# The square sums of the RMS norms and layer norms, taken with tokens on partitions and spread back to rows

## The reference, cut to what matters

```
def _rmsnorm(x, g):
    xf = x.astype(jnp.float32)
    xf = xf * lax.rsqrt(jnp.mean(xf * xf, axis=-1, keepdims=True) + EPS)
    return xf.astype(x.dtype) * g

def _layernorm(x, g, b):
    xf = x.astype(jnp.float32)
    mu = jnp.mean(xf, axis=-1, keepdims=True)
    xc = xf - mu
    var = jnp.mean(xc * xc, axis=-1, keepdims=True)
    return (xc * lax.rsqrt(var + EPS)).astype(x.dtype) * g + b
...
    for l in range(DEPTH):
        h = _rmsnorm(x, p["g_norm_mix"][l]) * (1 + scale_m) + shift_m
        m, st = _token_mixer(h, ...)          # its layer norm: conf = silu(_layernorm(conv, ...))
        x = x + gate_m * m
        h = _rmsnorm(x, p["g_norm_ffn"][l]) * (1 + scale_f) + shift_f
        f = _swiglu(h, ...) if l % 2 == 0 else _moe_swiglu(h, ...)
        x = x + gate_f * f
    y = _rmsnorm(x, p["g_final"])
```

## Time and profile before

| | |
|---|---|
| median of 3 runs | 1502.15 us (1499.78 to 1505.53) |
| the profiled execution: its own time, its span | 1501.98 us, 1500.2 us |
| PE busy | 1403.1 us, 94% of the span, 9312 products |
| PE weight loads busy | 1234.5 us, 82% |
| DVE busy | 1022.5 us, 68% |
| ACT busy | 785.6 us, 52% |
| DMA | 327.33 MB, mean 218 GB/s |
| granted clock of TensorE, mean | 0.968 of full speed |

### The profile page before, as it was taken

One profiled execution on the slowest core, in us unless ns is written; L12 is line 12 of the kernel. 1 busy time (PEld: TensorE's weight loads), 2 busy tenths in 40 slices (PEclk: granted clock), 3 DMA queues, 4 the chain that ended last, 5 costly groups with the idle time before them and its releaser, 6 DMA issues.

```text
span 1500.2 us, 24401 instructions
## 1 busy us (share of the span) xinstructions
PE 1403.1 (94%) x9312; PEld 1234.5 (82%) x9312; DVE 1022.5 (68%) x1417; ACT 785.6 (52%) x1062; POOL 38.2 (3%) x66
## 2 busy tenths in 40 slices
PE   5899999998889999998999999988899999999984
PEld 4788999875889999996989988767588888888863
DVE  2376999874554444334769987744788898889855
ACT  2534448634433333225443586243778788778852
POOL 0000100000000000000001000000200000000100
PEclk8999999999989999999999999999899999999996
DMA  9856743124446867434858661245689999999951
GB/s 310 228 169 197 235 141 125 59 85 154 135 140 201 255 217 237 177 100 121 246 159 290 198 186 57 85 140 188 223 320 386 383 387 388 378 386 385 384 203 68
DMA packets 280099, 327.33 MB, mean 218 GB/s; under 512 B 32319, under 2 KB 190471, under 8 KB 280007
## 3 DMA queue, kind: packets, MB, share of 16 engines
q1 hardware_dynamic: 273042, 314.29, 63.0%
q10 hardware_dynamic: 5492, 6.53, 1.3%
q0 software_dynamic: 1472, 5.24, 1.0%
HBM read 310.84 MB, written 15.17 MB: 217 GB/s over the span
## 4 chain that ended last, share of the span: by engine, by line
PE 88%; DVE 5%; ACT 2%; DMA 2%; SPq 1%; issue 1%; ACTq 0%; POOLq 0%; POOL 0%; DVEq 0%
PE mmp L819 14%; PE mmp L821 14%; PE mmp L820 13%; PE mmp L1221 8%; PE mmp L1223 8%; PE mmp L1222 8%; PE mmp L813 7%; PE py L789 2%; PE px L869 2%; PE py L885 1%; PE lg L985 1%; PE lg L869 1%; PE px L1027 1%; DVE hT L1796 1%; DMA ring<-in_w_ada_dram 1%
## 5 line engine op out<-in xcount | busy, mean ns | idle before, releaser
L819 PE MATMUL mmp<-hT_hi,wm_hi 128*128 128x320 f32 (+1 forms) x976 | 308.3, 316 | 13.1 <-DVE merged_lo L2023 5.1
L821 PE MATMUL mmp<-hT_hi,ring_lo 128*128 128x320 f32 (+1 forms) x976 | 306.2, 314 | 0.0
L820 PE MATMUL mmp<-hT_lo,wm_hi 128*128 128x320 f32 (+1 forms) x848 | 263.3, 310 | 0.0
L1827 DVE TENSOR_TENSOR ring_lo<-ring,wm_hi 128x1024 fp32r<-128x1024 f32 (+1 forms) x124 | 148.1, 1201 | 86.5 <-ACT wm_hi L1423 84.3
L819 PEld LDWEIGHTS mmp<-hT_hi,wm_hi 128*128 128x128 f32 (+1 forms) x976 | 184.7, 189 | 18.6 <-issue 8.4
L821 PEld LDWEIGHTS mmp<-hT_hi,ring_lo 128*128 128x128 f32 (+1 forms) x976 | 184.3, 189 | 0.2
L1423 ACT CAST wm_hi<-ring 128x1024 fp32r<-128x1024 f32 (+1 forms) x124 | 126.7, 1029 | 101.5 <-PE mmp L821 80.7
L820 PEld LDWEIGHTS mmp<-hT_lo,wm_hi 128*128 128x128 f32 (+1 forms) x848 | 159.3, 188 | 0.2
L1380 ACT ACTIVATE tmp<-mmp 128x320 f32<-128x320 f32 x70 | 30.7, 438 | 231.5 <-PE mmp L821 163.1
L1915 DVE SCALAR_TENSOR_TENSOR conv<-u_conf,dwc,conv 128x350 f32<-128x350 f32 x240 | 132.2, 581 | 3.1
L2048 DVE TENSOR_TENSOR wd_lo<-ring,wd_hi 128x2048 fp32r<-128x2048 f32 (+1 forms) x34 | 75.7, 2229 | 64.6 <-ACT wd_hi L1587 64.5
(11 more groups left out here) (371 smaller groups left out, 2866.2 us busy)
## 6 DMA issues: line engine op xcount, KB each, us to landing
ring<-in_w_in_dram SPq DMA_DIRECT2D x104, 512.0 KB, 4.6
ring<-in_w_exp_in_dram SPq DMA_DIRECT2D x64, 512.0 KB, 8.2
more<-in_w_exp_in_dram SPq DMA_DIRECT2D x64, 512.0 KB, 11.2
ring<-in_w_ada_dram SPq DMA_DIRECT2D x56, 512.0 KB, 7.2
more<-in_w_exp_out_dram SPq DMA_DIRECT2D x48, 512.0 KB, 6.9
ring<-in_w_ffn_in_dram SPq DMA_DIRECT2D x44, 512.0 KB, 5.9
wide<-in_w_ada_dram SPq DMA_DIRECT2D x40, 512.0 KB, 7.6
ring<-in_w_branch_dram SPq DMA_DIRECT2D x48, 256.0 KB, 2.8
```

Source lines behind the costliest of these rows:

```text
L819: nc.tensor.matmul(out, w_hi, x_hi, start=is_first, stop=False)
L820: nc.tensor.matmul(out, w_hi, x_lo, start=False, stop=False)
L821: return nc.tensor.matmul(out, w_lo, x_hi, start=False, stop=is_last)
L1827: V.tensor_tensor(mix_rows(ring_lo, l, s, r), mix_rows(ring, l, s, r), mix_hi(l, s, r).bitcast(F32), ALU.subtract).then_inc(mix_lo_ready, 1)
```

## The change

The sums are taken with tokens on partitions. For each squared block TensorE loads the squares as weights, for 64, 128 and 128 tokens in that order, and multiplies by one column of ones; the sums of 320 tokens stand in three columns of `py`. A product of zeros clears the columns first. ACT takes the root of these columns in two instructions (128x2 and 64x1), DVE the reciprocal of 128x3. Then TensorE spreads: for each column, it is repeated along the row as weights and multiplied by the identity, which gives `rstd` for each token on every partition, in PSUM (`rstd_rows`). DVE's multiplies read it there.

The spread of norm 0 stands behind the first transpose of the adaLN part; those of the others directly behind the sums. In the layer norm the spread stands ahead of chunk 2, and the multiply is moved behind the second merge. One memset on POOL is added at the start; `rstd` (1280 bytes on each partition) goes, and two tiles of 12 bytes come. `std` stays, as the router uses it.

```
+        sum_col = py[:, 0:3]
+        rstd_rows = py[:, P:P + T]
+        blocks_of = ((0, P), (P, P), (2 * P, TS))
...
+            nc.gpsimd.memset(std_col[:], 1.0)
...
+            def column_sums(squares, is_first, is_last):
+
+                if is_first:
+                    nc.tensor.matmul(sum_col, zeros[:, 0:P], zeros[:, 0:3], start=True, stop=False)
+                for t in (2, 0, 1):
+                    t0, m = blocks_of[t]
+                    ins = nc.tensor.matmul(py[0:m, t:t + 1], squares[:, t0:t0 + m], ones[:, 0:1],
+                                           start=False, stop=(is_last and t == 1))
+                return ins
+
+            def spread():
+
+                for t, (t0, m) in enumerate(blocks_of):
+                    ins = nc.tensor.matmul(rstd_rows[:, t0:t0 + m], rstd_col[0:m, t:t + 1].broadcast_to([m, P]),
+                                           ident[0:m, 0:m], start=True, stop=True)
+                return ins
...
-                    ins = nc.tensor.matmul(py[:, 0:T], ones[:], sq(k)[:, c, :], start=(c == 0), stop=(c == DC - 1))
+                    ins = column_sums(sq(k)[:, c, :], c == 0, c == DC - 1)
...
+            def norm_spread(k):
+                pe.wait_ge(rstd_ready, k + 1)
+                spread().then_inc(rstd_spread, 1)
...
             for m in range(ADA_FIRST):
                 ada_turn(0, m)
+                if m == 0:
+                    norm_spread(0)
...
                     norm_sums(2 * l)
+                    norm_spread(2 * l)
...
                     if j == 1:
                         pe.wait_ge(ln_sq, l + 1)
-                        group(py[:, 0:T], [(ones[:], hT[:, BC + c, :]) for c in range(BC)]).then_inc(ln_ss, 1)
+                        for c in range(BC):
+                            ins = column_sums(hT[:, BC + c, :], c == 0, c == BC - 1)
+                        ins.then_inc(ln_ss, 1)
+                    if j == 2:
+                        pe.wait_ge(ln_rstd, l + 1)
+                        spread().then_inc(ln_spread, 1)
...
+            def root_columns(n):
+                for m, c in ((P, slice(0, 2)), (TS, slice(2, 3))):
+                    ins = nc.scalar.activation(std_col[0:m, c], sum_col[0:m, c], ACT.Sqrt, scale=1.0 / n,
+                                               bias=eps[0:m, 0:1])
+                return ins
...
-                link(V.reciprocal(rstd[:], std[:]))
+                V.reciprocal(rstd_col[:], std_col[:]).then_inc(rstd_ready, 1)
...
             def norm_apply(k):
+                dve.wait_ge(rstd_spread, k + 1)
...
-                        V.tensor_tensor(hT[:, c, :], xT[:, c, :], rstd[:], ALU.mult).then_inc(xn_step, 1)
+                        V.tensor_tensor(hT[:, c, :], xT[:, c, :], rstd_rows, ALU.mult).then_inc(xn_step, 1)
...
-                        link(V.reciprocal(rstd[:], std[:]))
-                        V.tensor_tensor(hT[:, 0:BC, :], hT[:, 0:BC, :], bcast(rstd[:], BC, T),
+                        V.reciprocal(rstd_col[:], std_col[:]).then_inc(ln_rstd, 1)
+                    if j == 1:
+                        dve.wait_ge(ln_spread, l + 1)
+                        V.tensor_tensor(hT[:, 0:BC, :], hT[:, 0:BC, :], bcast(rstd_rows, BC, T),
                                         ALU.mult).then_inc(ln_n, 1)
```

More of the change, by code:

```diff
@@ L199, in build @@
         std = sb("std", [P, T])
-        rstd = sb("rstd", [P, T])
+        std_col = sb("std_col", [P, 3])
+        rstd_col = sb("rstd_col", [P, 3])
         vec = sb("vec", [P, DEPTH, NROWS])
@@ L408, in build @@
         std_ready = sem("std_ready")
+        rstd_ready = sem("rstd_ready")
+        rstd_spread = sem("rstd_spread")
         xn_step = sem("xn_step")
@@ L436, in build @@
         ln_std = sem("ln_std")
+        ln_rstd = sem("ln_rstd")
+        ln_spread = sem("ln_spread")
         ln_n = sem("ln_n")
@@ L1116, in _ @@
                 norm_sums(2 * l + 1, (DC - 2, DC - 1))
+                norm_spread(2 * l + 1)
                 if l % 2 == 0:
@@ L1278, in _ @@
             norm_sums(4)
+            norm_spread(4)
             pe.wait_ge(h_ready, DC * 5)
@@ L1345, in square @@
                 nc.scalar.activation(sq(k)[:, c, :], xT[:, c, :], ACT.Square).then_inc(sq_ready, 1)
+            def root_columns(n):
[3 more added lines that the diff above has]
+                return ins
             def norm_std(k):
                 act.wait_ge(sum_ready, k + 1)
-                nc.scalar.activation(std[:], py[:, 0:T], ACT.Sqrt, scale=1.0 / D,
-                                     bias=eps[:, 0:1]).then_inc(std_ready, 1)
+                root_columns(D).then_inc(std_ready, 1)
             def norm_scale(k, gain_of, shift_of):
@@ L1571, in _ @@
                         act.wait_ge(ln_ss, l + 1)
-                        nc.scalar.activation(std[:], py[:, 0:T], ACT.Sqrt, scale=1.0 / DB,
-                                             bias=eps[:, 0:1]).then_inc(ln_std, 1)
+                        root_columns(DB).then_inc(ln_std, 1)
                 act.wait_ge(ln_n, l + 1)
```

## The result

The changed kernel takes **1522.14 us** in the median of 4 runs (1517.64 to 1523.41), the kernel before beside it 1503.38 (1499.78 to 1505.53): a ratio of 1.0126, 95% interval 1.0107 to 1.0146. It is slower by 18.8 us. The profiled execution took 1523.36 us with a span of 1521.6, so the two profiled executions lie 21.4 us apart.

The account below looks back on a forecast made before the run. TensorE was taken as the bound (88% of the chain). Norms 1, 2, 3, 4, the layer norms and norm 0 summed as 1.4+4.4+2.3+2.9+5.7+2.0 = 18.7 us on 1502.0, forecast 1521; range over all cases 1503 to 1527.

Parts of the forecast that it names:

- A block of sums: Square sums of 128x320 on TensorE: three products in six passes, 0.76 us at full clock for 0.54, 1.27 at half.
- Second rival: Changing tile shape between the sums' weight loads costs nothing: +10 us in all, 1512 us; chance 0.12.
- The spread: TensorE's repeating of rstd along rows: six passes and one change of shape, 0.95 us at full clock, 1.6 at half.
- norm 4: Norm ahead of the last transposes: sums at half clock take 10.8 us against 7.36, chain 0.5 shorter, +2.9 us.
- Layer norms: Inside each mixer, twice: longer sums and spread in TensorE's queue, reciprocal already free; +2.85 us each, 5.7 in all.
- Norm 2: Norm ahead of layer 1's qkv: clock falls to half during the sums, +4.4 us, bounds +0.7 and +6.
- norm 1: Norm ahead of the feed-forward: sums between output chunks lengthen the queue, last pair partly at half clock; +1.4 us.
- norm 3: Norm ahead of the experts: sums between output chunks lengthen the queue, last pair at half clock; +2.3 us.
- Norm 0: Norm ahead of layer 0's qkv, beside first weight loads: DMA wait hides it at full clock, up to +5; taken +2.
- The first rival: At the norms, narrow one-column products hold TensorE's clock at full: +6.1 us, 1508 us; chance 0.15.
- The third: Rival of other sign: shorter, broken idle stretch behind each norm keeps the clock at 2.4 GHz; -6.6 us, 1495; chance 0.05.
- The fourth: Rival: weight loads in sums and spreads keep their speed at half clock; +8 us, 1510 us; chance 0.10.

Follow-up runs that it names:

- the kernel with 128 columns: Changed kernel whose products of the squares each stream 128 columns of ones instead of one, one sum column being read: 1520.44 us, ratio 1.0100 to before.
- the filled one: Changed kernel with products of zeros that nobody reads put into TensorE's queue where it waits: 1516.91 us, ratio 1.0086 to the kernel before.
- the kernel with one tile shape: Changed kernel whose third column takes tokens 192 to 319, so all loads are 128 wide: 1515.81 us, ratio 1.0077 to the kernel before.

## Why the prediction was right

The forecast was 1521, slower; it is 1522.14, and the reason is the one that was given: the new form lengthens TensorE's queue and takes away time of DVE that nobody waited for at the two layer norms and at norm 0. Term by term, with what the trace shows:

- **Root and reciprocal.** 0.40 and 0.18 us, forecast 0.41 and 0.164; the multiply from PSUM costs nothing (482 ns in the median). Right.
- **A block of sums.** Forecast 0.76 at full clock and 1.27 at half; measured from start to start of a block 0.74 and 1.24. The tile shape was taken as 0.10 a change. At full clock the loads of one shape start 0.11 apart and those of 64 columns 0.055, and at the two changes the gap is 0.207 and 0.151: 0.10 more each, as taken. Second rival out.
- **The spread.** From the reciprocal's end to the multiply 1.16 us at full clock (the kernel with 128 columns) and 1.93 at half, forecast 0.95 and 1.6. Sized too small by 0.2 and 0.3. Its one change of shape is most of that: the load behind it starts 0.311 us after the one ahead of it at full clock and 0.558 at half, where 0.11 and 0.21 are usual, so the change costs 0.20 and 0.34 and not the 0.10 taken from narrow products. So the chain wins 0.9 at full clock (root's start to multiply 2.75 before, 1.86) and 0.2 at half (2.54 in norm 4).
- **Layer norms.** Sums 3.11 us from 335.90 to 339.01, forecast 3.26. Layer norm 0 shifts what follows by 2.0 and layer norm 1 by 4.2 in the profile, 6.2 in all for a forecast of 5.7 (2.0 and 2.3 in the kernel that has the new form in the layer norms alone); the stretches at half clock that the one-column sums bring on (339.7 to 343.1) and those that go from behind the silu's wait decide between the two.
- **Norm 2** 4.0 and up to 5.0 with what follows (forecast 4.4), **norm 1** 1.8 to 2.2 (1.4), **norm 3** +1.6 up to the row product (2.3), **norm 4** 3.2 and 3.7 to the end (2.9).
- **Norm 0** is the term that was mis-sized: 3.2 us are left in the attention branch, forecast 2. Its sums took 8.95 us from 20.68, since they fall to half clock too, where 26.5 had been taken for their end at full and 2 us for the mixture of both; the spread ended at 32.2, and the wait for DMA that was to hide it was used up. One pair of executions says little here: the start of the attention branch of layer 0 comes 0.8 to 3.4 us later than in the profile of before in the three kernels that have this norm 0 (the changed one, its layer norms as before, its idle time filled), and 0 to 3.2 earlier in the six that have the old one. The averages lie 4.4 us apart, twice the forecast.

So the sum of 18.7 stands against 18.8 by the medians, but against 21.4 in the profiled executions from which the terms were taken: norm 0 and the second layer norm were each some 1.3 us too small there. Of the two only norm 0 is too small across several traces; the second layer norm and the others are within what a stretch at half clock moves. That the medians agree to 0.1 us is luck: single runs of the changed kernel lie 6 us apart.

**The first rival** (narrow products hold the clock; 1508) is refuted twice: by norm 2 of the changed kernel and by the filled one, where they begin at full clock, follow 1.4 us of idleness and end at half. **The third** (the clock stays up behind the norms; 1495) is refuted by the window of 688 to 692 at 0.50; it is 0.50 too from there to the first wide product at 694.22 and up to 698. **The fourth** (loads keep their speed at half clock; 1510) is refuted by the loads themselves. The instructions of the sums' line in norm 4 of the kernel with one tile shape, duration in ns as min/median/max:

```profile
L896 PEld LDWEIGHTS py<-ones,ring x48: 192/333/333, 1490.2 to 1499.0; 128*128 128x128 f32 x48
```

A load lasts 192 ns at full clock and 333 at half, and loads start 0.112 and 0.213 us apart. The Trainium skill ("TensorE: Matmul & The Clock Gate", section "LDWEIGHTS (loading the stationary operand)") gives a load the time of its columns divided by 1.2, 0.107 us for 128 columns, and names no clock with it. The spacing at full clock, 0.112, nearly agrees; that at half, 0.213, is twice the rule's.

What stays open: how wide a stream must be to hold the clock (1 column didn't, 128 did), and why the clock differs more from run to run in some kernels. The time follows it: the kernels with 128 columns scatter over 11 us (0.968 to 0.978 of full speed in the mean) and 15 (0.978 to 0.988), the one before over 7 (0.965 to 0.970).

## What to carry to other kernels

A reduction over partitions by a product with ones costs TensorE its columns; turned around, in this kernel it costs two weight loads per 64 or 128 tokens of each block, which one streamed column does not hide. Where TensorE is the bound, price the loads (and each change of tile shape), and ask of the work that is taken from DVE whether anybody waited for it: at the two layer norms nobody did, and they carry 5.4 to 8.6 of the 18.8 us by the medians. Read the granted clock in the stretch of the narrow products as well as behind them, because they bring it down and everything up to the next dense stretch pays. And where a kernel of this kind waits for a short chain of other engines, products of zeros into an unread bank are worth trying: 0.6% here, where no form of the norms gave anything.

## What the runs showed of the hardware that was not expected

- A queue of one-column f32 products with loads of 64 and 128 columns, PE busy in each window, let the clock fall from 2.4 to 1.2 GHz while it ran (0.79, then 0.50); the same queue with 128 columns did not (1.00).
- Nine products of zeros (18 passes of 256 columns, 4.05 us) kept the clock at 2.4 GHz from 668 to 680 us across norm 2, where it had been down in the kernel before.
- A clock that is at half when 128-column products begin need not rise in 14.26 us of them (norm 4 without filling). In the same place with filling it rose 1.8 us after they had begun, and under 320-column products within 7.36. What decides between these was not tested.
- A change of tile shape between f32 products costs 0.10 us at full clock when they stream one column, and 0.20 when they stream 128 (the spread, and the kernel with 128 columns).
